# The last granule of the last MLP with tokens in rows, normed and stored block by block

## The chip, the cores and the metric

One core of one Trainium2 chip runs the whole program. The metric is the device time of one execution in microseconds. A difference is told here in microseconds and in per cent of the time before.

## What is computed

Two transformer-like stacks on 512 tokens of 1024 features, all in float32. The end of it, cut to what matters here, for the last layer:

```python
def rmsnorm(x, g):
    y = x * lax.rsqrt(jnp.mean(x * x, axis=-1, keepdims=True) + EPS)
    return y * g

def sq_relu_mlp(hn, w1, w2):          # w1: 1024 x 4096, w2: 4096 x 1024
    return jnp.square(jax.nn.relu(hn @ w1)) @ w2

h = h + sq_relu_mlp(rmsnorm(h, norm_mlp_g[l]), mlp_w1[l], mlp_w2[l])
return rmsnorm(h, final_norm_g)       # out: 512 tokens x 1024 features
```

## The kernel before

Every product is made three times: each operand is split in a high part (rounded to the fp32r type by ACT) and a low part (the rest, by DVE or POOL), and PE adds high x high, low x high, high x low in a PSUM bank (`split_sum`, L529 to L531).

**Layout.** The residual `x` (named `resid` in the trace) lies with features in rows: 8 tiles of 128 features x 512 tokens. The eight PSUM banks are four tile banks, used in turn, two `s_bank`, `pt_bank` (also `col_bank`) and `o_bank` (also `stat_bank`).

**The MLP.** The 4096 inner features are worked in 8 granules of 512. A granule is two up halves (`by_feature`, two tiles of 24 products each), whose result DVE scales (L1760) and ACT squares twice (L2270 into `t_buf`, L2271 as `g_hi`), and DVE subtracts (`g_lo`, L1175). Then `down` multiplies the granule back: first the quarter of the weights for output tiles 0 to 3, then the one for tiles 4 to 7, each tile 12 products. DVE adds each bank into `x` (L1223). All PE work for up half n+1 runs ahead of `down` for granule n.

**Weights.** SP loads them in chunks of 1 MB, in turn into the two slots of `raw`. ACT converts a chunk to `w_hi` in two pieces (`split_high`, L1921), DVE makes `w_lo` of the first piece (L1161) and, in this part of the program, POOL of the second (L499). `w_hi` and `w_lo` have two slots as well: chunk c may be converted only when PE is done with chunk c-2. For the last down quarter, that is the last up half.

**The end.** After each of the last `down`'s tiles, ACT squares the residual (L1933) and multiplies it by the final gain into `y_final` (L1946), and DVE adds up the squares (`add_squares`, L1792). Then `last_stat` sums them over the features on PE by a product with ones (L1107, L1112), ACT takes the root (L1954), DVE the reciprocal (L1886). `turned` transposes `y_final` on PE into eight banks of 128 tokens x 512 features (L1127), DVE and ACT scale four each into `out_stage` (L1892, L2348), and SP stores in four pieces of 512 KB (L416).

The order on each engine is the order of the code; engines meet by semaphores alone.

Of the kernel before, what the change touches and what calls it, by code (L numbers as in the profile page):

```python
# [14 lines left out]
P = 128  # L15
# [127 lines left out]
def build(nc, w, out):  # L143
# [5 lines left out]
    with ExitStack() as ctx:  # L149
# [3 lines left out]
        def sem(name):  # L153
            return ctx.enter_context(nc.semaphore(name))
# [56 lines left out]
        rope_a, rope_b = at(20480, S), at(20992, S)  # L211
        y_final, out_stage = at(4096, KT, S), at(8192, TT, D)
        OUT_PIECES = [(half, t) for half in range(2) for t in range(TT)]
        causal = biases.rearrange("p a b -> p (a b)")
# [71 lines left out]
        gm_ready = sem("gm_ready")  # L286
        y_ready = sem("y_ready")
        last_sq = sem("last_sq")
# [3 lines left out]
        out_scalar = sem("out_scalar")  # L292
        stored = sem("stored")
# [13 lines left out]

        def out_banks(tiles):

            four = [tile_bank[(tiles + q) % 4] for q in range(4)]  # L310
            return four + [s_bank[0], s_bank[1], o_bank, four[0]]

# [74 lines left out]
        def _(sp):  # L387
# [22 lines left out]

            for k in range(4):
                half, t = OUT_PIECES[2 * k]
                sp.wait_ge(out_vector, k + 1)
                sp.wait_ge(out_scalar, k + 1)
                cut = slice(512 * half, 512 * half + 512)
                sp.dma_start(out.rearrange("(t p) n -> p t n", p=P)[:, t:t + 2, cut], out_stage[:, t:t + 2, cut])\  # L416
                  .then_inc(stored, 16)
            sp.wait_ge(stored, 16 * 4)

# [83 lines left out]
        def _(pe):  # L503
# [40 lines left out]

            def by_feature(tiles=2, moving=None, arrive=None, first=0, pair=False, between=None):

                wait_chunk()
                for j in range(first, tiles):
                    dst = next_bank()[:]
                    parts = (range(0, 5), range(5, KT)) if j == 1 and between else (range(KT),)  # L550
# [475 lines left out]

            def mlp():
# [71 lines left out]
            back(3)  # L1099
            mlp()  # L1100

            def last_stat():

                pe.wait_ge(acc_ready, stats.n + 1)
                pe.wait_ge(std_done, stats.n)
                for t in range(TT):
                    nc.tensor.matmul(col_bank[:, t:t + 1], sq[:, 0, P * t:P * t + P], ones[:, 0:1], start=(t == 0), stop=False)  # L1107
                turned(0)
                for t in range(TT):
                    if t % 2 == 0:  # L1110
                        pe.wait_ge(last_sq, t // 2 + 1)
                    last = nc.tensor.matmul(col_bank[:, t:t + 1], sq[:, KT - 1, P * t:P * t + P], ones[:, 0:1],  # L1112
                                            start=False, stop=(t == TT - 1))
                last.then_inc(stat_full, 1)
                stats.n += 1

            def turned(q):

                half, t = OUT_PIECES[q]
                if t == 0:  # L1120
                    pe.wait_ge(y_ready, 4 * half + 4)
                if q < 4:
                    pe.wait_ge(tile_taken, tile.n - 3 + q + (q == 3))
                elif q == 7:
                    pe.wait_ge(out_vector, 1)
                for n in range(4):
                    last = nc.tensor.transpose(out_banks(tile.n)[q][:, P * n:P * n + P],  # L1127
                                               y_final[:, 4 * half + n, P * t:P * t + P], ident[:])
                last.then_inc(out_full, 1)

            last_stat()
            for q in range(1, len(OUT_PIECES)):
                turned(q)


        @block.vector
        def _(dve):
# [615 lines left out]
            def mlp(following):  # L1753
# [20 lines left out]
                if following:  # L1774
                    down(following)
                    return
                for n in range(KT - 1):
                    back_tile(n)
                    if n >= 2:
                        add_squares(n - 1)  # L1780
                add_squares(KT - 2)
                dve.wait_ge(tile_full, tile.n + 1)
                for cut in (slice(0, 256), slice(256, 512)):
                    ins = V.tensor_tensor(x[:, KT - 1, cut], tile_bank[tile.n % 4][:, cut], x[:, KT - 1, cut], ALU.add)
                    ins.then_inc(tile_taken, 1)
                tile.n += 1

            def add_squares(n):

                dve.wait_ge(sq_done, sq_n.n + n + 1)  # L1790
                settle()
                ins = V.tensor_tensor(sq[:, 0, :], sq[:, 0, :], sq[:, n, :], ALU.add)  # L1792
                if n < KT - 2:
                    keep_order(ins)
                else:
                    ins.then_inc(acc_ready, 1)

# [85 lines left out]

            stats.n += 1
            dve.wait_ge(std_done, stats.n)
            V.reciprocal(rstd_col[:, 0:4], rstd_col[:, 0:4]).then_inc(t_made, 1)  # L1886
            made.n += 1
            dve.wait_ge(t_made, made.n)
            for q in range(0, len(OUT_PIECES), 2):
                half, t = OUT_PIECES[q]  # L1890
                dve.wait_ge(out_full, q + 1)
                V.tensor_scalar(out_stage[:, t, 512 * half:512 * half + 512], out_banks(tile.n)[q][:],  # L1892
                                rstd_col[:, t:t + 1], None, ALU.mult).then_inc(out_vector, 1)


        @block.scalar
        def _(act):
# [41 lines left out]
            def prep(n, name, s=None):  # L1939
# [4 lines left out]
                squares(sq if s is None else s, n, x[:, n, :])  # L1944
                if not name:
                    A(y_final[:, n, :], x[:, n, :], ACT.Copy, scale=gain("final_norm_g_2", n)).then_inc(y_ready, 1)  # L1946

# [21 lines left out]
            def down(last=False, name=None, then=lambda: None):  # L1969

                for n in range(KT):
                    if last and not name and n == KT - 1:
                        for j in range(2):
                            cut = slice(256 * j, 256 * j + 256)
                            if j == 0:
                                taken()
                            else:
                                act.wait_ge(tile_taken, tile.n + 1)
                            A(sq[:, n, cut], x[:, n, cut], ACT.Square).then_inc(last_sq, 1)
                        A(y_final[:, n, :], x[:, n, :], ACT.Copy, scale=gain("final_norm_g_2", n)).then_inc(y_ready, 1)  # L1980
                    elif last:
# [282 lines left out]
            def mlp(following):  # L2264
                root(rstd[:, 0, :], None, stat_bank[:], None, D)

                def up(granule):
                    for j in range(2):
                        taken()
                        A(t_buf[:, j, :], r_buf[:, j, :], ACT.Square)  # L2270
# [6 lines left out]
                for n in range(7):  # L2277
                    down()
                    up(0)
                    up(1)  # L2280
                    if following and n == 5:
                        for j, table in enumerate((rope_cos, rope_sin)):
# [3 lines left out]
                            acts.n += 1  # L2286
                down(True, following)

# [49 lines left out]
            tile.n += 24  # L2338
            back(True, "mlp1")
            mlp(None)  # L2340

            root(None, rstd_col[:, 0:4], None, col_bank[:, 0:4], D)
            made.n += 1
            act.wait_ge(t_made, made.n)
            for q in range(1, len(OUT_PIECES), 2):
                half, t = OUT_PIECES[q]
                act.wait_ge(out_full, q + 1)
                A(out_stage[:, t, 512 * half:512 * half + 512], out_banks(tile.n)[q][:], ACT.Copy,  # L2348
                  scale=rstd_col[:, t:t + 1]).then_inc(out_scalar, 1)

# [40 lines left out]
```

## Time and profile before

| | us |
|---|---|
| median of 3 runs | 2001.6 |
| lowest, highest | 1999.96, 2001.6 |
| profiled execution | 1999.41 |
| its span | 1997.7 |
| PE busy | 1979.9 (99%) |
| DVE busy | 1162.7 (58%) |
| ACT busy | 756.3 (38%) |
| POOL busy | 247.9 (12%) |

A 128x512 matmul record is 0.39 us long, but the next one starts well before it ends, so records overlap and PE counts as busy throughout. Times in the timeline are microseconds from the start of the span, first the start, then the duration (of a merged group: from its first start to its last end). `PEclk` is the granted clock of TensorE, 1.00 being 2.4 GHz.

### The profile page before, as it was taken

The page shows a single profiled execution, that of the slowest core. Times are in us where ns is not written, and L with a number is a line of the kernel's source. Part 1 is how long each engine was busy: PE and PEld are TensorE (multiplying, and loading weights), DVE is VectorE, ACT ScalarE, POOL GpSimd, SP SyncE. Part 2 cuts the span into 40 slices and gives each one's busy share as a digit, 9 for nine tenths or more (in the row PEclk, how much of TensorE's full clock was granted, in tenths as well). Part 3 has the DMA queues.
Part 4 walks back from the last instruction along what each step waited for, and adds up shares of the span by engine and source line. Part 5 has one row for each costly group of instructions (what it writes and reads, how often), then busy time and mean ns, then how long its engine had stood idle before and what let it go on. Part 6 is the DMA issues. An engine that isn't in the chain of part 4 may idle for free.

```text
span 1997.7 us, 23016 instructions
## 1 busy us (share of the span) xinstructions
PE 1979.9 (99%) x9343; PEld 1623.4 (81%) x9343; DVE 1162.7 (58%) x1677; ACT 756.3 (38%) x1191; POOL 247.9 (12%) x189
## 2 busy tenths in 40 slices
PE   9999999999999999999999999999999999999998
PEld 7877777888888888888888888888877778888887
DVE  6665687577665656647577444443587674333334
ACT  5453554344333333533324323223443353232224
POOL 1001440000000000000001132222211012222221
PEclk9999999999999999999999999999999999999999
DMA  5322212113232322332222322323232013323321
GB/s 178 107 79 85 85 64 85 64 64 106 85 106 86 105 93 99 105 98 93 92 79 88 106 95 95 105 88 102 74 93 92 22 43 106 106 84 106 103 87 63
DMA packets 138713, 180.51 MB, mean 90 GB/s; under 512 B 9712, under 2 KB 97392, under 8 KB 138608
## 3 DMA queue, kind: packets, MB, share of 16 engines
q1 hardware_dynamic: 136720, 177.52, 27.3%
q8 instruction: 74, 1.21, 0.3%
q10 hardware_dynamic: 1632, 1.51, 0.2%
q14 instruction: 31, 0.25, 0.0%
q0 software_dynamic: 256, 0.02, 0.0%
HBM read 176.91 MB, written 2.10 MB: 90 GB/s over the span
## 4 chain that ended last, share of the span: by engine, by line
PE 94%; DVE 3%; issue 1%; ACT 1%; DMA 0%; POOL 0%; SPq 0%; ACTq 0%; POOLq 0%; DVEq 0%
PE bank L529 26%; PE bank L531 26%; PE bank L530 26%; PE bank L693 4%; PE bank L572 2%; PE bank L574 2%; PE bank L573 2%; PE bank L685 1%; PE bank L783 1%; PE bank L771 1%; PE bank L998 1%; DVE w_lo L1161 1%; DVE arena L1200 1%; PE bank L775 0%; DVE h_lo L1177 0%
## 5 line engine op out<-in xcount | busy, mean ns | idle before, releaser
L529 PE MATMUL bank<-h_hi,w_hi 128*128 128x512 f32 x1384 | 546.3, 395 | 0.0
L531 PE MATMUL bank<-h_hi,w_lo 128*128 128x512 f32 x1384 | 539.0, 389 | 0.0
L530 PE MATMUL bank<-h_lo,w_hi 128*128 128x512 f32 x1384 | 538.7, 389 | 0.0
L1921 ACT ACTIVATE w_hi<-raw 128x1024 fp32r<-128x1024 f32 (+2 forms) x335 | 331.2, 1031 | 507.6 <-PE bank L531 452.2
L529 PE MATMUL bank<-g_hi,w_hi 128*128 128x512 f32 (+1 forms) x972 | 377.1, 388 | 1.4 <-issue 0.7
L531 PE MATMUL bank<-g_hi,w_lo 128*128 128x512 f32 (+1 forms) x972 | 371.8, 383 | 0.0
L530 PE MATMUL bank<-g_lo,w_hi 128*128 128x512 f32 (+1 forms) x972 | 371.4, 382 | 0.0
L499 POOL TENSOR_TENSOR w_lo<-raw,w_hi 128x1024 fp32r<-128x1024 f32 (+1 forms) x75 | 181.9, 2426 | 1491.5 <-ACT w_hi L1921 1491.5
L1161 DVE TENSOR_TENSOR w_lo<-raw,w_hi 128x1024 fp32r<-128x1024 f32 (+2 forms) x258 | 308.9, 1221 | 60.2 <-ACT w_hi L1921 59.5
L1223 DVE TENSOR_TENSOR resid<-bank,resid 128x512 f32<-128x512 f32 x287 | 194.2, 688 | 224.9 <-PE bank L531 224.3
L529 PEld LDWEIGHTS bank<-h_hi,w_hi 128*128 128x128 f32 x1384 | 259.8, 188 | 56.3 <-issue 3.2
L530 PEld LDWEIGHTS bank<-h_lo,w_hi 128*128 128x128 f32 x1384 | 259.9, 188 | 55.8 <-issue 2.9
L531 PEld LDWEIGHTS bank<-h_hi,w_lo 128*128 128x128 f32 x1384 | 259.8, 188 | 54.4
L529 PEld LDWEIGHTS bank<-g_hi,w_hi 128*128 128x128 f32 x972 | 182.7, 188 | 39.3 <-issue 4.0
L531 PEld LDWEIGHTS bank<-g_hi,w_lo 128*128 128x128 f32 x972 | 182.6, 188 | 35.8
L530 PEld LDWEIGHTS bank<-g_lo,w_hi 128*128 128x128 f32 x972 | 182.8, 188 | 34.2 <-issue 0.2
L1760 DVE SCALAR_TENSOR_TENSOR arena<-bank,rstd 128x512 f32<-128x512 f32 x64 | 44.0, 691 | 179.0 <-PE bank L531 178.8
L2270 ACT ACTIVATE arena<-arena 128x512 f32<-128x512 f32 x64 | 40.5, 633 | 225.9 <-DVE arena L1760 225.9
L2012 ACT ACTIVATE arena<-bank 128x128 f32<-128x128 f32 (+3 forms) x104 | 44.7, 430 | 138.4 <-PE bank L685 137.8
L1175 DVE TENSOR_TENSOR g_lo<-arena,g_hi 128x512 fp32r<-128x512 f32 x112 | 74.9, 688 | 22.2 <-ACT g_hi L2271 20.6
L693 PE MATMUL bank<-arena 128*128 128x128 f32 (+2 forms) x448 | 84.0, 326 | 1.7 <-ACT arena L2029 0.9
L693 PEld LDWEIGHTS bank<-arena 128*128 128x128 f32 x448 | 66.6, 191 | 18.3 <-issue 5.6
(244 smaller groups left out, 1794.6 us busy)
## 6 DMA issues: line engine op xcount, KB each, us to landing
raw<-w SPq DMA_DIRECT2D x64, 1024.0 KB, 5.2
raw<-w_up SPq DMA_DIRECT2D x22, 1024.0 KB, 5.1
raw<-a_w_in SPq DMA_DIRECT2D x16, 1024.0 KB, 5.3
raw<-w_in SPq DMA_DIRECT2D x11, 1024.0 KB, 5.3
raw<-w_down SPq DMA_DIRECT2D x11, 1024.0 KB, 5.0
raw<-w_mkv SPq DMA_DIRECT2D x8, 1024.0 KB, 5.2
raw<-a_w_out SPq DMA_DIRECT2D x8, 1024.0 KB, 5.0
raw<-w_out SPq DMA_DIRECT2D x4, 1024.0 KB, 5.1
```

Source lines behind the costliest of these rows:

```text
L499: G.tensor_tensor(lo, src, hi.bitcast(F32), ALU.subtract).then_inc(w_split_pool, 1)
L529: nc.tensor.matmul(dst, a_hi, b_hi, start=(k == 0), stop=False)
L530: nc.tensor.matmul(dst, a_hi, b_lo, start=False, stop=False)
L531: last = nc.tensor.matmul(dst, a_lo, b_hi, start=False, stop=(k == n - 1))
L693: ins = nc.tensor.matmul(dst, a, b, start=first, stop=last)
L1161: V.tensor_tensor(lo, src, hi.bitcast(F32), ALU.subtract).then_inc(w_split, 1)
L1175: V.tensor_tensor(lo, src, hi.bitcast(F32), ALU.subtract).then_inc(ready, 1)
L1223: take(lambda b: V.tensor_tensor(x[:, n, :], b[:], x[:, n, :], ALU.add))
L1760: take(lambda b: V.scalar_tensor_tensor(r_buf[:, j, :], b[:], 0.0, rstd[:, 0, :], ALU.max, ALU.mult))
L1921: A(hi, src, ACT.Copy).then_inc(w_hi_done, 1)
L2012: A(prob_t_of(kind, u)[:, 0:nk], pt_bank[:, 0:nk], ACT.Copy).then_inc(pt_taken, 1)
L2270: A(t_buf[:, j, :], r_buf[:, j, :], ACT.Square)
```

## The change

1. The last granule's `down` is replaced by `last_granule`. The products have tokens in rows: `g` (128 tokens) is the stationary operand, 512 columns of the weights move. There are eight banks, block t of 128 tokens x half of the features, 12 products each; blocks 0 and 1 are made in two passes over the inner features, blocks 2 and 3 in one. Before its first product PE waits for both quarters' low parts.
2. The residual, which is complete up to the granule before, is turned on PE ahead of it (`residual`): 16 transposes between the two tiles of the last up half, 16 after them. ACT copies each bank into `x_rows`, four copies ahead of the second tile of the last up half and four after the last conversion of weights.
3. The end is done for each block of 128 tokens: DVE adds bank and `x_rows`, and multiplies by the gain; ACT squares the sum with `accum_out`, takes the root; DVE takes the reciprocal, scales and releases the store.
4. The gain comes in by its own DMA, spread over all partitions, on ACT's queue ahead of the last MLP. SP stores three blocks of 512 KB and the last in two of 256 KB.
5. The sums of squares on PE, `y_final`, the transposes at the end and ACT's scaling go.

```diff
+            def residual(first):
+                if first == 0:
+                    pe.wait_ge(std_done, stats.n)
+                    pe.wait_ge(tile_taken, tile.n - 3)
+                else:
+                    pe.wait_ge(x_rows_taken, 4)
+                for q in range(4):
+                    for n in range(4):
+                        last = nc.tensor.transpose(free_banks[q][:, P * n:P * n + P],
+                                                   x[:, 4 * (q % 2) + n, P * (first + q // 2):P * (first + q // 2) + P], ident[:])
+                    last.then_inc(x_turned, 1)
+            def last_granule():
+                def products(t, half, ks):
+                    dst, slot = out_bank(tile.n, t, half)[:], (chunk.n + half) % 2
+                    for k in ks:
...
+                        nc.tensor.matmul(dst, a_hi, b_hi, start=(k == 0), stop=False)
+                        nc.tensor.matmul(dst, a_hi, b_lo, start=False, stop=False)
+                        last = nc.tensor.matmul(dst, a_lo, b_hi, start=False, stop=(k == 3))
...
+                pe.wait_ge(w_split, by_vector(chunk.n + 2))
+                pe.wait_ge(w_split_pool, by_pool(chunk.n + 2))
+                for ks in ((0, 1), (2, 3)):
+                    for t in range(2):
+                        for half in range(2):
...
+                            products(t, half, ks)
+                for t in range(2, TT):
+                    for half in range(2):
+                        pe.wait_ge(x_rows_taken, 2 * t + half + 1)
+                        products(t, half, range(4))
...
-                    by_feature()
-                    down()
+                    by_feature(between=lambda: residual(0), first_part=KT) if last and n == 6 else by_feature()
+                    if last and n == 6:
+                        residual(2)
+                        last_granule()
+                    else:
+                        down()
...
# DVE, in place of add_squares, the reciprocal and four scalings
+            for t in range(TT):
+                for half in range(2):
+                    dve.wait_ge(out_full, 2 * t + half + 1)
...
+                    V.tensor_tensor(out_stage[:, t, cut], out_bank(tile.n, t, half)[:], x_rows[:, t, cut],
+                                    ALU.add).then_inc(last_added, 1)
...
+                    V.tensor_tensor(x_rows[:, t, cut], out_stage[:, t, cut],
+                                    last_gain[...], ALU.mult).then_inc(last_scaled, 1)
+                    if half == 0:
+                        dve.wait_ge(row_squared, 2 * t + 1)
+                        V.tensor_scalar(row_means[:, t:t + 1], row_sums[:, 2 * t:2 * t + 1], 1.0 / D, EPS, ...)
+                dve.wait_ge(row_std, t + 1)
+                keep_order(V.reciprocal(row_stds[:, t:t + 1], row_stds[:, t:t + 1]))
+                settle()
+                for half in range(2):
+                    V.tensor_scalar(out_stage[:, t, cut], x_rows[:, t, cut], row_stds[:, t:t + 1], None, ALU.mult)
...
# ACT
+                def rows_of_x(first):
+                    for q in range(4):
+                        act.wait_ge(x_turned, 2 * first + q + 1)
+                        A(x_rows[:, first + q // 2, cut], free_banks[q][:], ACT.Copy).then_inc(x_rows_taken, 1)
...
+                    A(last_squares[:, half, :], out_stage[...], ACT.Square, accum_out=row_sums[:, q:q + 1])
+                A(row_stds[:, t:t + 1], row_sums[:, 2 * t + 1:2 * t + 2], ACT.Sqrt, scale=1.0 / D,
+                  bias=row_means[:, t:t + 1]).then_inc(row_std, 1)
```

PE at the end of the last up half and the start of the last granule, before (L529 to L531 are the three products; `h` is the up half's operand, `g` the granule's):

```order
L529 MATMUL bank<-h_hi,w_hi 128x512
L530 MATMUL bank<-h_lo,w_hi 128x512
L531 MATMUL bank<-h_hi,w_lo 128x512
L529 MATMUL bank<-g_hi,w_hi 128x512
L530 MATMUL bank<-g_lo,w_hi 128x512
L531 MATMUL bank<-g_hi,w_lo 128x512
```

The same place now (L536 to L538 are the three products of the up half, L1045 the transposes, L1058 to L1060 the granule's products):

```order
L536 MATMUL bank<-h_hi,w_hi 128x512
L537 MATMUL bank<-h_lo,w_hi 128x512
L538 MATMUL bank<-h_hi,w_lo 128x512
L1045 MATMUL bank<-ident,resid 128x128 x16
L1058 MATMUL bank<-w_hi,g_hi 128x512
L1059 MATMUL bank<-w_lo,g_hi 128x512
L1060 MATMUL bank<-w_hi,g_lo 128x512
```

Sixteen transposes stand between the last up tile and the granule (the other sixteen one tile earlier), and the granule's first product has `g` stationary.

ACT from the last up half on, before (the waits are named in brackets; L1921 is the conversion of weights):

```order
L2270 ACTIVATE arena<-arena 128x512 [waits tile_taken]
L2271 ACTIVATE g_hi<-arena 128x512
L1921 ACTIVATE w_hi<-raw 128x1024 [waits tile_full,w_loaded1]
L1921 ACTIVATE w_hi<-raw 128x1024
L1933 ACTIVATE arena<-resid 128x512 [waits tile_taken]
L1946 ACTIVATE arena<-resid,vec 128x512
```

And now (L1934 is the conversion, L2273 the copies of turned residual, L2363 the squares, L2367 the root):

```order
L2273 ACTIVATE arena<-bank 128x512 [waits x_turned] x4
L2280 ACTIVATE arena<-arena 128x512 [waits tile_taken]
L2281 ACTIVATE g_hi<-arena 128x512
L1934 ACTIVATE w_hi<-raw 128x1024 [waits tile_full,w_loaded1]
L1934 ACTIVATE w_hi<-raw 128x1024
L2273 ACTIVATE arena<-bank 128x512 [waits x_turned] x4
L2363 ACTIVATE arena,rstd_col<-arena 128x512 [waits last_added] x2
L2367 ACTIVATE rstd_col<-rstd_col,small 128x1 [waits mean_ready,row_squared]
```

The conversion of the last chunk stands where it stood, with four copies ahead of the second tile's squares and four behind it.

DVE for one block of tokens, now (L1890 is the sum, L1893 the gain, L1898 the mean of the first half, L1906 the scalings):

```order
L1890 TENSOR_TENSOR arena<-bank,arena 128x512 [waits x_rows_taken,out_full]
L1893 TENSOR_TENSOR arena<-arena 128x512 [waits last_added]
L1898 TENSOR_SCALAR small<-rstd_col 128x1 [waits row_squared]
L1890 TENSOR_TENSOR arena<-bank,arena 128x512 [waits x_rows_taken,out_full]
L1893 TENSOR_TENSOR arena<-arena 128x512 [waits last_added]
L1901 RECIPROCAL rstd_col<-rstd_col 128x1 [waits row_std]
L1906 TENSOR_SCALAR arena<-arena,rstd_col 128x512 [waits last_scaled,own]
L1906 TENSOR_SCALAR arena<-arena,rstd_col 128x512 [waits last_scaled]
```

These eight stand four times, in place of the eight sums into `resid`, the sums of squares and four scalings from banks.

## Rows read from the trace of the kernel before

**Rows 1.** The page: span, and busy time of the engines.
```profile
span 1997.7 us, 23016 instructions
PE 1979.9 (99%) x9343; PEld 1623.4 (81%) x9343; DVE 1162.7 (58%) x1677; ACT 756.3 (38%) x1191; POOL 247.9 (12%) x189
```

**Rows 2.** Timeline of PE, first product of the last granule: start, us, what.
```profile
1964.93 0.39 PE L529 MATMUL bank<-g_hi,w_hi 128*128 128x512 f32 x1
```

**Rows 3.** Timeline of PE, last product, and the sums behind it.
```profile
1986.46 0.40 PE L531 MATMUL bank<-g_hi,w_lo 128*128 128x512 f32 x1
1986.69 0.95 PE L1107 MATMUL bank<-ones,arena 128*128 128x1 f32 x8
...
1987.97 0.95 PE L1112 MATMUL bank<-ones,arena 128*128 128x1 f32 x8
```

**Rows 4.** Chain of waits in order of time, its end: start, us, what.
```profile
1988.92 3.13 PE bank L1127 x28
...
1992.08 0.69 ACT arena L2348
```

**Rows 5.** Timeline of PE, transposes between products near the start.
```profile
14.40 0.39 PE L531 MATMUL bank<-h_hi,w_lo 128*128 128x512 f32 x1
14.63 0.60 PE L726 MATMUL bank<-ident,arena 128*128 128x128 f32 x4
...
15.30 0.39 PE L530 MATMUL bank<-h_lo,w_hi 128*128 128x512 f32 x1
```

**Rows 6.** Timelines of SP, ACT, DVE and POOL, the last chunk's load and split.
```profile
1948.10 0.37 SPq L409 DMA_DIRECT2D raw<-w  x1
...
1960.95 0.62 ACT L2271 ACTIVATE g_hi<-arena 128x512 fp32r<-128x512 f32 x1
...
1965.13 0.69 DVE L1760 SCALAR_TENSOR_TENSOR arena<-bank,rstd 128x512 f32<-128x512 f32 x1 [4.75 <-PE bank L531]
...
1966.91 1.99 ACT L1921 ACTIVATE w_hi<-raw 128x1024 fp32r<-128x1024 f32 x2
...
1968.98 2.48 POOL L499 TENSOR_TENSOR w_lo<-raw,w_hi 128x1024 fp32r<-128x1024 f32 x1 [8.39 <-ACT w_hi L1921]
```

**Rows 7.** Groups by line and shape, PE: weights moving: count, busy us, mean ns.
```profile
L572 PE MATMUL bank<-w_hi,h_hi 128*128 128x512 f32 x192 | 77.1, 401 | 0.0
```

**Rows 8.** Timeline of DVE: independent operations, then two that depend on each other.
```profile
1977.10 0.68 DVE L1223 TENSOR_TENSOR resid<-bank,resid 128x512 f32<-128x512 f32 x1
1977.70 0.68 DVE L1792 TENSOR_TENSOR arena<-arena 128x512 f32<-128x512 f32 x1
...
1544.62 0.15 DVE L1276 RECIPROCAL small<-small 128x1 f32<-128x1 f32 x1
1544.81 0.49 DVE L1278 TENSOR_SCALAR arena<-arena,small 128x512 f32<-128x512 f32 x1
```

**Rows 9.** ACT: timeline of a square with its sum; groups: root on one column.
```profile
27.30 1.04 ACT L2044 ACTIVATE arena<-arena 128x1024 f32<-128x1024 f32 x1
28.25 0.18 ACT L2044 ACTIVATION_READ_ACCUMULATOR arena<-arena 128x1 f32 x1
...
L2050 ACT ACTIVATE rstd_col<-small 128x1 f32<-128x1 f32 x1 | 0.2, 202 | 0.0
```

**Rows 10.** Line L416, the stores: issue to landing of the first, of the last.
```profile
DMA to landing us min/median/max: 2.8/2.8/2.8
DMA to landing us min/median/max: 4.4/4.4/4.4
```

**Rows 11.** Windows at the end: length, busy of each engine, clock, DMA share, GB/s.
```profile
1994.50:1995.40 0.90, 0.00 (x0) 0.00 (x0) 0.00 (x0) 0.00 (x0) 0.00 (x0) 1.00 1.01 373
...
1995.80:1997.70 1.90, 0.00 (x0) 0.00 (x0) 0.00 (x0) 0.00 (x0) 0.00 (x0) 0.50 0.50 190
```

**Rows 12.** Timeline of PE, the program's first records, and the same ones later.
```profile
1.34 3.78 PE L699 MATMUL bank<-ones 128*128 128x128 f32 x16 [1.34 <-POOL ones L430]
...
7.34 1.06 PE L699 MATMUL bank<-ones 128*128 128x128 f32 x8
```

More of the change, by code:

```diff
@@ L211, in build @@
         rope_a, rope_b = at(20480, S), at(20992, S)
-        y_final, out_stage = at(4096, KT, S), at(8192, TT, D)
-        OUT_PIECES = [(half, t) for half in range(2) for t in range(TT)]
+        last_gain, last_squares, out_stage, x_rows = at(4096, KT, P), at(5120, 2, S), at(8192, TT, D), at(12288, TT, D)
+        row_sums, row_means, row_stds = rstd_col[:, 4:12], small[:, 32:36], rstd_col[:, 0:4]
         causal = biases.rearrange("p a b -> p (a b)")
@@ L306, in gain, with out_bank @@
             return vec[:, c:c + 1]
-        def out_banks(tiles):
-            four = [tile_bank[(tiles + q) % 4] for q in range(4)]
-            return four + [s_bank[0], s_bank[1], o_bank, four[0]]
+        free_banks = [s_bank[0], s_bank[1], pt_bank, o_bank]
+        def out_bank(tiles, t, half):
+            last_four = [tile_bank[(tiles + q) % 4] for q in range(4)]
+            return (last_four + free_banks)[2 * t + half]
         UNITS = [(h, i) for h in range(8) for i in range(TT)]
@@ L543, in w_tiles, with by_feature @@
                 return [(view(w_hi, slot)[:, k, cut], view(w_lo, slot)[:, k, cut]) for k in range(n)]
-            def by_feature(tiles=2, moving=None, arrive=None, first=0, pair=False, between=None):
+            def by_feature(tiles=2, moving=None, arrive=None, first=0, pair=False, between=None, first_part=5):
                 wait_chunk()
@@ L549, in by_feature @@
                     dst = next_bank()[:]
-                    parts = (range(0, 5), range(5, KT)) if j == 1 and between else (range(KT),)
+                    parts = (range(0, 5), range(5, KT)) if j == 1 and between and first_part < KT else (range(KT),)
+                    if j == 1 and first_part == KT:
+                        between()
                     for part in parts:
@@ L1099, in _ @@
             back(3)
[L1100 to L1133, printed above, removed]
+            mlp(last=True)
         @block.vector
@@ L1775, in mlp @@
                     down(following)
[L1776 to L1796, printed above, removed]
             mlp("mix1")
@@ L1971, in down @@
                 for n in range(KT):
[L1972 to L1981, printed above, removed]
+                    if last:
                         taken()
@@ L2279, in mlp @@
                     up(0)
-                    up(1)
+                    up(1, last=not following and n == 6)
                     if following and n == 5:
@@ L2286, in mlp @@
                             acts.n += 1
[L2287 removed]
+                if following:
+                    down(True, following)
+                else:
+                    rows_of_x(2)
             act.dma_start(pos_i.bitcast(I32), w["positions_2"].partition_broadcast(P)).then_inc(pos_loaded, 16)
@@ L2339, in _ @@
             back(True, "mlp1")
+            first = sum(n for _, n in VECTORS[2][:-1])
+            act.dma_start(last_gain, w["vectors"][first:first + KT, 2, :].partition_broadcast(P)).then_inc(gain_loaded, 16)
             mlp(None)
[L2342 to L2349, printed above, removed]
+            for t in range(TT):
+                for half in range(2):
+                    q = 2 * t + half
+                    act.wait_ge(last_added, q + 1)
+                    if q >= 2:
+                        act.wait_ge(row_squared, q - 1)
+                    A(last_squares[:, half, :], out_stage[:, t, 512 * half:512 * half + 512], ACT.Square,
+                      accum_out=row_sums[:, q:q + 1]).then_inc(row_squared, 1)
+                act.wait_ge(row_squared, 2 * t + 2)
+                act.wait_ge(mean_ready, t + 1)
+                A(row_stds[:, t:t + 1], row_sums[:, 2 * t + 1:2 * t + 2], ACT.Sqrt, scale=1.0 / D,
+                  bias=row_means[:, t:t + 1]).then_inc(row_std, 1)
 def kernel(**inputs):
```

64 lines of the change are left out of this document (40 added, 24 removed).

## The prediction

> **What bounds the kernel now.** I read the page first: the span is 1997.7 us and PE is busy for 99% of it [rows 1], so a matmul added or a stall of PE costs its whole length, unless it falls after the last product. The change touches only the last granule and what follows, so the next view was the timeline of the end. There PE starts the last granule's products at 1964.93, in the slot right behind the last product of the second up half [rows 2], and its last product ends at 1986.46 + 0.40 = 1986.86 [rows 3]. What follows is a tail: squares, 32 transposes, root, reciprocal, scaling, four stores, until 1997.7. Tail: 10.84 us. The chain of waits gives the tail's first part to PE's own short matmuls (3.13 us for 28 transposes) and leaves ACT last, at 1992.77 [rows 4]. The rest is the store.
>
> The profiled execution took 1999.41 us, 1.71 more than its span; the median shown is 2001.6. I work out the difference on the span and add it to 2001.6.
>
> **Term 1, the transposes ahead of the granule.** 32 transposes of the residual now stand in the stream: 16 between the two tiles of the last up half, 16 behind them. Before, 32 stood in the tail, so their count is the same, only their place is new. The price between products is read at the start of the trace: from product 14.40 to product 15.30 there are 0.90 us for one product slot, four transposes and another slot [rows 5]; a slot is 0.2265 us (21.76 us from the first product at 1964.93 [rows 2] to what follows the last at 1986.69 [rows 3], over 96), so four transposes cost 0.447 us, 0.112 each. The last 28 in the tail say the same, 3.13 / 28 = 0.112 [rows 4]. Each 16 cost 1.78 us. The first 16 stand squarely on the path. Of the second 16 see term 2.
>
> **Term 2, a new wait for the second weight quarter.** Before, PE starts on the first quarter (512 of the 1024 output features) and needs the second only 48 products later, at 1964.93 + 48 x 0.2265 = 1975.8. In the new order the second quarter comes with the seventh product, and both waits stand ahead of the first, so PE waits for both to be split before it begins. The second quarter's weights have been loaded long since (issued 1948.10 [rows 6]), but its high part is written over the slot of the last up chunk, so ACT may not begin before the last up tile is done. [Rows 6] are that chain: tile taken by DVE at 1965.13, two squares on ACT, two conversions from 1966.91 to 1968.90, and POOL's low piece from 1968.98 to 1971.46. Before, this ended 4.3 us ahead of its use; now it is the last thing PE waits for. Everything in the chain hangs on the last up tile, which comes 1.78 later, so PE's first product starts at 1971.46 + 1.78 + 0.03 = 1973.27. That is 8.34 after 1964.93: 3.56 are the 32 transposes and 4.78 are idle slots. The second 16 transposes are therefore free, as they lie inside this wait; if the wait went, they would cost 1.78.
>
> ACT has four copies (bank to SBUF) ahead of the last up tile. It has time: the first tile's squares end at 1960.95 + 0.62 = 1961.6 [rows 6], four copies of at most 0.7 us (ACT's last operation, bank to SBUF too, took 0.69 [rows 4]) end by 1964.4, and the next tile comes at 1966.9. The other four stand behind the two conversions, off POOL's chain; they end by 1973.5, before their first use 10.9 us into the products.
>
> **Term 3, the products.** 96 products before, 96 after. The tokens are now the stationary operand, the weights move. The same form ran in the earlier projections, at a mean of 401 ns a record with the stage's own starts in it [rows 7], against 0.39 us a record here [rows 2]. I price it at the same 0.2265 a slot. The last product's record ends at 1973.27 + 95 x 0.2265 + 0.39 = 1995.18, which is 8.32 later than before.
>
> **Term 4, DVE beside the products.** For each token block DVE now adds twice, multiplies by the gain twice, makes one small sum, one reciprocal and two scalings; ACT squares twice with a row sum and takes one root. From rows: add or multiply 0.69 (0.61 from start to start where nothing is waited for), reciprocal 0.15, scaling from SBUF 0.49, and 0.04 between dependent instructions [rows 8]; a square of 512 columns 0.62 [rows 6], the read of a square's sum 0.18, overlapping it by 0.09, and a root on one column 0.20 [rows 9]. A block's first half takes 0.73 + 0.77 until the sum is there + 0.07 = 1.57 on DVE; its second half takes 0.73 + 0.77, root 0.22, reciprocal 0.20, scalings 0.85: 2.77. Together 4.34. The first four banks fill at 7.0, 8.35, 9.7 and 11.05 us after the first product, the others at 13.8, 16.5, 19.2 and 21.95. DVE starts at 7.0 and is free for the last bank at 7.0 + 3 x 4.34 + 1.57 = 21.6. It is ready 0.35 ahead of PE, no more. So three blocks hide beside the products and only the last half's chain is left, but every 0.1 us more per block uses that up.
>
> **Term 5, the new tail.** From the last product's end: 0.03, add 0.69, 0.03, square and its sum 0.71, 0.04, root 0.20, 0.04, reciprocal 0.15, 0.04, scalings 0.49 + 0.41 = 2.83. Then the store. Before, the first store of 512 KB, with nothing ahead of it, landed 2.8 after issue; the last, behind three others, 4.4, and the span ended 0.5 after it [rows 10]. The queues moved about 380 GB/s [rows 11], so 512 KB take 1.37 and the fixed part is 1.43. The new last store has 256 KB (0.68) behind another 256 KB issued 0.41 ahead of it: 1.43 + 0.68 + 0.27 = 2.4. Bounds: 2.1 with nothing ahead, 4.4 as the last store of before took, which had 1.5 MB ahead of it; I stay near the first. New tail: 2.83 + 0.05 + 2.4 + 0.5 = 5.8, against 10.84: 5.06 less.
>
> **Sum.** +8.32 - 5.06 = +3.26: the span comes to about 2001.0 and the median to 2004.8. The saved tail is real, but the wait for the split costs more.
>
> **The gain's load** (512 KB, on ACT's queue ahead of the last MLP) costs nothing: it is issued where ACT next waits for PE's sum of squares, and ACT is busy for 38% of the span [rows 1]. Without that cover it would be one issue, 0.37 us on SP [rows 6].
>
> **The clock.** PE's new gap is 4.6 us between records. The one fall of the granted clock in the trace stands at the end: PE's last work ends at 1992.05 [rows 4], the clock is 1.00 until 1995.4 and 0.50 from 1995.8 on [rows 11], so it fell 3.4 to 3.7 us after. The gap is longer than that.
> The Trainium skill (TensorE: Matmul & The Clock Gate, Part 4: PE-mode transpose) says that transposes do not count as PE-busy for the clock gate. By that rule the second 16 transposes would lengthen the quiet stretch to 6.4 us and the fall would be near certain. The trace speaks against it: nothing but transposes ran after 1988.92 [rows 3, 4], and the clock was full for another 6.5 us. So I leave the rule out of the sum; by it the time would be that of the first rival.
>
> **The rivals.**
> - *The clock falls in the new gap.* PE restarts at 1.2 GHz instead of 2.4. What a slow stretch looks like is seen at the start: 16 records from 1.34 take 3.78 us, 8 of the same from 7.34 take 1.06 [rows 12], so it is half rate, for some 4.4 us of work until about 5.7. Half of 4.4 is lost: 2.2, bounds 1 and 3.5. For it: the gap exceeds the 3.7 us within which it fell. Against: that is one observation, and the margin is 0.9 us. +5.5 in all: 2007.0, slower by more than 0.2%. This is the case on the other side of the bound, and it decides once the fall comes before 1973.3.
> - *DVE is late for the last bank.* If dependent steps take 0.1 to 0.15 longer than my rows (the row sum on a square, the waits on an instruction of the same engine), a block takes some 4.8, the last add begins 1.1 late and the last chain is 0.3 longer: +1.4, 2006.2.
> - *The wait does not come*, because the second quarter is split sooner or taken later than I read. Then the idle slots go and the 32 transposes alone delay the products: 3.26 - 4.78 = -1.5, 2000.1. Against it: both waits stand ahead of the first product, and the slot is the last up chunk's.
>
> **How the numbers follow.** Less than 0.2%, 4 us here, can't be told from no change. Forecast 0.50, clock 0.33, DVE late 0.10, no wait 0.07. The forecast lies only 0.8 below the bound of 4; a fifth of its chance is beyond it (0.10), of the clock's five sixths (0.28), of DVE's six tenths (0.06): slower 0.44. Faster by over 0.2% would need 7 us less than the forecast, more than the wait and the doubt of the store together: 0.02. Same: 0.54. The likeliest case alone spans 2003.4 to 2006.0; the range, 2002.2 to 2008.4, takes in the clock's case up to 3.5 lost.
>
> **What would show it.** PE idle for 4.5 to 4.8 us behind the second 16 transposes, with POOL's low piece named as what ended it; 96 products in 21.75 us behind it; granted clock 1.00 through (or 0.50 for some us: the first rival); the last product to the end of the span in 5.8 us; DVE idle for some tenths before its last add. Wrong would be: a wait under 3 us, a slot over 0.2265 in the new form at full clock, a last store over 3 us to land.

## The result, and the profile after

| | before | after |
|---|---|---|
| median, us | 2001.6 (14 runs) | 2006.74 (14 runs) |
| lowest, highest | 1999.56, 2001.9 | 2005.13, 2007.38 |
| profiled execution, its span | 1999.41, 1997.7 | 2007.1, 2005.3 |

The ratio is 1.0027, 95% interval 1.0021 to 1.0034: slower by 0.27%, or 5.1 us between medians. That is more than the 3.2 of the forecast and nearly the 5.5 of the first rival; 2006.74 lies in the range.

The timeline of the changed kernel, PE and the engines it waits for, from the last up tile on (start, duration, what, and in brackets the idle time before it and what ended it):

```profile
1969.00 1.91 PE L1045 MATMUL bank<-ident,resid 128*128 128x128 f32 x16
...
1969.20 0.69 DVE L1781 SCALAR_TENSOR_TENSOR arena<-bank,rstd 128x512 f32<-128x512 f32 x1 [6.52 <-PE bank L538]
...
1970.98 1.99 ACT L1934 ACTIVATE w_hi<-raw 128x1024 fp32r<-128x1024 f32 x2
...
1973.04 2.43 POOL L506 TENSOR_TENSOR w_lo<-raw,w_hi 128x1024 fp32r<-128x1024 f32 x1 [10.18 <-ACT w_hi L1934]
...
1975.58 0.77 PE L1058 MATMUL bank<-w_hi,g_hi 128*128 128x512 f32 x1 [4.67 <-issue]
1976.14 0.63 PE L1059 MATMUL bank<-w_lo,g_hi 128*128 128x512 f32 x1
...
1979.56 0.60 PE L1058 MATMUL bank<-w_hi,g_hi 128*128 128x512 f32 x1
1979.98 0.41 PE L1059 MATMUL bank<-w_lo,g_hi 128*128 128x512 f32 x1
...
1999.29 0.39 PE L1060 MATMUL bank<-w_hi,g_lo 128*128 128x512 f32 x1
```

They answer to [rows 6] and [rows 2, 3]. Behind the second 16 transposes PE is idle for 4.67 us. The page puts this down to "issue", that is, to nothing it can show, but POOL's low piece ends at 1973.04 + 2.43 = 1975.47, 0.11 before PE starts. Then the records are 0.63 long and 0.43 apart, until 1980.0, where they fall back to 0.39 and 0.23. The windows name the cause (the column before the last two is the granted clock):

```profile
1966.00:1969.00 3.00, 3.00 (x15) 2.40 (x15) 0.00 (x0) 0.00 (x0) 0.00 (x0) 1.00 0.00 0
1969.00:1973.10 4.10, 1.91 (x17) 1.67 (x15) 3.03 (x4) 3.18 (x5) 0.06 (x1) 1.00 0.00 0
1973.20:1979.90 6.70, 4.32 (x10) 3.47 (x11) 0.08 (x1) 1.71 (x4) 2.28 (x1) 0.50 0.01 2
1980.00:1999.00 19.00, 19.00 (x85) 15.73 (x84) 12.47 (x26) 5.61 (x16) 0.00 (x0) 1.00 0.14 59
```

The clock fell in the gap, and the first ten products ran at 1.2 GHz. From the start of the first product to that of the last are 23.71 us; 95 slots of 0.2265 are 21.52. The clock cost 2.19. How much of a low clock is paid depends on how much of it lies beside work: it was low for 6.8 us here, 2.4 of them still in the gap.

The end of the changed kernel, timeline of ACT, DVE and SP for the last half of the last block:

```profile
1999.72 0.69 DVE L1890 TENSOR_TENSOR arena<-bank,arena 128x512 f32<-128x512 f32 x1 [0.18 <-PE bank L1060]
...
2000.44 0.63 ACT L2363 ACTIVATE arena<-arena 128x512 f32<-128x512 f32 x1 [1.10 <-DVE arena L1890]
...
2000.98 0.19 ACT L2363 ACTIVATION_READ_ACCUMULATOR arena<-arena 128x1 f32 x1
2001.20 0.29 ACT L2367 ACTIVATE rstd_col<-rstd_col,small 128x1 f32<-128x1 f32 x1
2001.52 0.17 DVE L1901 RECIPROCAL rstd_col<-rstd_col 128x1 f32<-128x1 f32 x1 [0.39 <-ACT rstd_col L2367]
2001.72 0.88 DVE L1906 TENSOR_SCALAR arena<-arena,rstd_col 128x512 f32<-128x512 f32 x2
2002.24 0.81 SPq L424 DMA_DIRECT2D out<-arena  x2
```

The line of the last stores gives `2.0/2.2/2.3` us from issue to landing for 256 KB each, against 2.8 to 4.4 for 512 KB each in [rows 10]. From the end of PE's last record (1999.68) to the end of the span are 5.6 us, 10.84 before.

The profiled execution carries one thing more that is not the change's. PE reaches the last up tile 2.3 us later than in the profile of before, with 1.78 of transposes taken off: the clock fell once more, near 232 us, in a stretch that both kernels share. Windows there, the kernel before and the changed one:

```profile
232.00:240.00 8.00, 6.76 (x38) 5.07 (x39) 7.66 (x12) 4.70 (x14) 4.32 (x8) 1.00 0.40 132
...
232.40:239.20 6.80, 6.04 (x20) 4.27 (x21) 5.36 (x8) 2.25 (x6) 2.42 (x5) 0.50 0.46 154
```

Up to 231 us the changed kernel's DVE is 0.4 us behind that of before, from 245 us on it is 2.3 behind: 0.4 was there already and 1.9 came with the fall. So traces are compared from a point behind it: from DVE's taking of the last up tile to the end of the span, before 1997.7 - 1965.13 = 32.57, after 2005.3 - 1969.20 = 36.10, and 1.78 for the transposes ahead of it. **The change costs 5.31 us**: 8.36 for the later start of the products (predicted 8.34), 2.19 for the clock, and 5.24 won in the tail (predicted 5.06).

### The profile page after: what moved, and what is told of

Its sections match the earlier page's. It is cut to its first block, busy times and chain, and to the rows that moved or that the text cites. A ratio compares the mean times of both kernels' runs of the same rounds, so it can differ in the third digit from the quotient of the medians.

```text
span 2005.3 us, 23011 instructions
## 1 busy us (share of the span) xinstructions
PE 1983.8 (99%) x9327; PEld 1625.7 (81%) x9327; DVE 1166.2 (58%) x1689; ACT 754.4 (38%) x1197; POOL 244.9 (12%) x189
## 4 chain that ended last, share of the span: by engine, by line
PE 94%; DVE 3%; issue 1%; ACT 1%; POOL 0%; ACTq 0%; DVEq 0%; POOLq 0%
PE bank L536 25%; PE bank L538 25%; PE bank L537 25%; PE bank L702 4%; PE bank L581 2%; PE bank L583 2%; PE bank L582 2%; PE bank L694 1%; PE bank L792 1%; PE bank L780 1%; PE bank L1007 1%; DVE w_lo L1182 1%; DVE arena L1221 1%; PE bank L784 1%; PE bank L1058 0%
## 5 line engine op out<-in xcount | busy, mean ns | idle before, releaser
L536 PE MATMUL bank<-h_hi,w_hi 128*128 128x512 f32 x1384 | 546.3, 395 | 0.2 <-DVE h_lo L1198 0.2
L538 PE MATMUL bank<-h_hi,w_lo 128*128 128x512 f32 x1384 | 539.1, 390 | 0.0
L1934 ACT ACTIVATE w_hi<-raw 128x1024 fp32r<-128x1024 f32 (+2 forms) x335 | 331.2, 1031 | 507.2 <-PE bank L538 452.1
L536 PE MATMUL bank<-g_hi,w_hi 128*128 128x512 f32 (+1 forms) x940 | 364.6, 388 | 1.4 <-issue 0.7
L538 PE MATMUL bank<-g_hi,w_lo 128*128 128x512 f32 (+1 forms) x940 | 359.3, 382 | 0.0
L537 PE MATMUL bank<-g_lo,w_hi 128*128 128x512 f32 (+1 forms) x940 | 359.0, 382 | 0.0
L1244 DVE TENSOR_TENSOR resid<-bank,resid 128x512 f32<-128x512 f32 x280 | 189.5, 688 | 217.0 <-PE bank L538 216.2
L536 PEld LDWEIGHTS bank<-h_hi,w_hi 128*128 128x128 f32 x1384 | 259.9, 188 | 56.6 <-issue 3.6
L538 PEld LDWEIGHTS bank<-h_hi,w_lo 128*128 128x128 f32 x1384 | 259.7, 188 | 54.5
L536 PEld LDWEIGHTS bank<-g_hi,w_hi 128*128 128x128 f32 x940 | 176.7, 188 | 38.0 <-issue 4.0
L538 PEld LDWEIGHTS bank<-g_hi,w_lo 128*128 128x128 f32 x940 | 176.6, 188 | 34.6
L537 PEld LDWEIGHTS bank<-g_lo,w_hi 128*128 128x128 f32 x940 | 176.8, 188 | 33.0 <-issue 0.2
```

Source lines behind the costliest of these rows:

```text
L536: nc.tensor.matmul(dst, a_hi, b_hi, start=(k == 0), stop=False)
L537: nc.tensor.matmul(dst, a_hi, b_lo, start=False, stop=False)
L538: last = nc.tensor.matmul(dst, a_lo, b_hi, start=False, stop=(k == n - 1))
L1244: take(lambda b: V.tensor_tensor(x[:, n, :], b[:], x[:, n, :], ALU.add))
L1934: A(hi, src, ACT.Copy).then_inc(w_hi_done, 1)
```

## The experiments

In the table, "distance" is that from DVE's taking of the last up tile to the end of the span, and "net" is distance + 1.78 - 32.57, the part of the change and its variant in that one trace. Each value of distance and net is from one trace. Ratios are against runs of the kernel before on the same chip: the first four variants against 33 runs with a median of 2001.16, the last three against 27 with 2001.01.

| kernel | distance | net | median, ratio and interval |
|---|---|---|---|
| the change | 36.10 | +5.3 | 2006.74, 1.0027 (1.0021 to 1.0034) |
| first quarter first | 29.13 | -1.7 | 1998.60, 0.9988 (0.9980 to 0.9997) |
| gap filled, products | 34.13 | +3.3 | 2004.37, 1.0015 (1.0006 to 1.0024) |
| gap filled, transposes | 34.03 | +3.2 | 2004.11, 1.0015 (1.0006 to 1.0024) |
| low piece by DVE | 34.34 | +3.6 | 2004.04, 1.0018 (1.0009 to 1.0027) |
| wait at the seventh | 34.30 | +3.5 | 2004.71, 1.0018 (1.0009 to 1.0027) |
| first quarter first, no transposes | 28.66 | -3.9 (without 1.78) | 1997.38, 0.9983 (0.9974 to 0.9992) |
| first quarter first, early fill | 29.13 | -1.7 | 1997.79, 0.9986 (0.9977 to 0.9994) |

### The first quarter first

```diff
-                pe.wait_ge(w_split, by_vector(chunk.n + 2))
-                pe.wait_ge(w_split_pool, by_pool(chunk.n + 2))
-                for ks in ((0, 1), (2, 3)):
+                pe.wait_ge(w_split, by_vector(chunk.n + 1))
+                pe.wait_ge(w_split_pool, by_pool(chunk.n + 1))
+                for half in range(2):
+                    if half == 1:
+                        pe.wait_ge(w_split, by_vector(chunk.n + 2))
+                        pe.wait_ge(w_split_pool, by_pool(chunk.n + 2))
                     for t in range(2):
-                        for half in range(2):
...
-                            products(t, half, ks)
+                        pe.wait_ge(tile_taken, tile.n - 3 + 2 * t + half)
+                        products(t, half, range(4))
```

DVE waits for the banks in their new order.

> The changed kernel, with the granule's products in another order: the first quarter's columns of blocks 0 and 1 first (24 products, 5.4 us), waiting for the first quarter alone, then a wait for the second quarter and their other columns; blocks 2 and 3 as before. Theory A (the wait for POOL's low piece and the clock that falls in it are the loss): PE's gap behind the second 16 transposes goes, the second quarter is ready before its product, the clock is 1.00 there; 4.8 + 2.2 us less than the changed kernel, so about 1.5 us under the kernel before. Theory B (the loss lies in the products with weights moving, or in DVE's chain beside them): within 1 us of the changed kernel.

Its timeline of PE and POOL:

```profile
1968.27 1.91 PE L1045 MATMUL bank<-ident,resid 128*128 128x128 f32 x16
...
1969.93 0.47 PE L1058 MATMUL bank<-w_hi,g_hi 128*128 128x512 f32 x1
...
1972.33 2.50 POOL L506 TENSOR_TENSOR w_lo<-raw,w_hi 128x1024 fp32r<-128x1024 f32 x1 [10.19 <-ACT w_hi L1935]
...
1991.58 0.39 PE L1060 MATMUL bank<-w_hi,g_lo 128*128 128x512 f32 x1
```

The products start in the transposes' next slot and run through in 21.65 us; POOL ends at 1974.83, 0.6 ahead of the 25th product. Net -1.7 where -1.5 was expected. The changed kernel's whole loss, and a little more, lay in the wait and in what the clock did in it. Theory B is out: the new form of the products and the new end are the same here. Against the kernel before, the median is 0.12% less and the ratio's interval ends at 0.9997, just under 1: faster, at the edge of what the runs can tell.

### The gap filled with products, and with transposes

```diff
+                pe.wait_ge(tile_taken, tile.n - 3)
+                for _ in range(19):
+                    nc.tensor.matmul(out_bank(tile.n, 0, 0)[:, 0:P], ones[:], ones[:], start=True, stop=True)
                 pe.wait_ge(w_split, by_vector(chunk.n + 2))
```

(in the other run `for _ in range(38): nc.tensor.transpose(out_bank(tile.n, 0, 0)[:, 0:P], x[:, 0, 0:P], ident[:])`)

> The changed kernel, with 19 products of ones (128 columns, two records each, 4.2 us) put on PE between the second 16 transposes and the wait for the split, into a bank that the granule overwrites. Theory A: the wait ends when it did, the clock stays at 2.4 GHz, the products take 21.75 us from first to last slot and the time falls by the clock's 2.2 us. Theory B (the slow start of the products has another cause, such as new weights or the stage's start): no change from the changed kernel, or 0 to 0.3 us more.

> As the run with 19 products of ones, with 38 transposes of 128 columns (4.3 us) in their place. Theory A (PE's work of any kind holds the clock, as the 28 transposes at the end of the kernel before seemed to): clock 1.00, 2.2 us less than the changed kernel. Theory C (transposes do not count for the clock, as the page on TensorE says, and the clock fell since the last product had ended 4 us before): the clock falls as in the changed kernel, no gain.

Timeline of PE with products as filler:

```profile
1969.02 4.41 PE L1066 MATMUL bank<-ones 128*128 128x128 f32 x38
1973.87 0.47 PE L1058 MATMUL bank<-w_hi,g_hi 128*128 128x512 f32 x1 [0.44 <-issue]
...
1995.53 0.39 PE L1060 MATMUL bank<-w_hi,g_lo 128*128 128x512 f32 x1
```

and with transposes, with the clock of the products' start:

```profile
1969.12 4.31 PE L1066 MATMUL bank<-ident,resid 128*128 128x128 f32 x38
1973.98 0.47 PE L1058 MATMUL bank<-w_hi,g_hi 128*128 128x512 f32 x1 [0.56 <-issue]
```

```profile
1969.00:1973.80 4.80, 4.43 (x41) 4.19 (x39) 1.92 (x2) 4.28 (x7) 2.37 (x1) 1.00 0.01 3
1973.90:1980.00 6.10, 6.02 (x27) 5.02 (x28) 0.00 (x0) 0.00 (x0) 0.00 (x0) 1.00 0.00 0
```

Both hold the clock; the products run in 21.66 us, and the net is +3.3 and +3.2. That is the forecast's own case, +3.26, with the clock taken out of it: the wait alone costs what I had worked out, and the clock 2.0 to 2.1 on top. Theory B and theory C are both out. The rule of the Trainium skill (TensorE: Matmul & The Clock Gate, Part 4: PE-mode transpose), that transposes do not count as busy, does not hold for these: from the last product of the up half to the first of the granule are 6.4 us with transposes alone in them, and the clock stayed at 2.4 GHz. A second sign is in the times: the changed kernel's fourteen runs lie between 2005.13 and 2007.38, the 22 filled ones, in another series, between 2003.31 and 2005.17.

### The last low piece by DVE

```diff
-        SHARED = [c >= NOT_SHARED and c not in MLA_OUT for c in range(len(CHUNKS))]
+        SHARED = [c >= NOT_SHARED and c not in MLA_OUT and c < len(CHUNKS) - 1 for c in range(len(CHUNKS))]
```

> The changed kernel, with the second low piece of the last chunk on DVE and not on POOL. Theory A: DVE makes it from 0.08 before its first piece ends, in 1.23 us, 1.1 us ahead of POOL; PE's gap shrinks from 4.7 to 3.6 us and the time by 1.1 if the clock still falls, by 3.3 if it no longer does. Theory B (something else ends the wait): no change.

Timelines of DVE and PE, and the window of low clock:

```profile
1969.72 2.36 DVE L1182 TENSOR_TENSOR w_lo<-raw,w_hi 128x1024 fp32r<-128x1024 f32 x2 [0.25 <-ACT w_hi L1934]
...
1972.13 0.80 PE L1058 MATMUL bank<-w_hi,g_hi 128*128 128x512 f32 x1 [3.56 <-DVE w_lo L1182]
```

```profile
1971.80:1975.10 3.30, 2.97 (x7) 2.41 (x8) 0.28 (x1) 0.78 (x2) 0.00 (x0) 0.50 0.00 0
```

The gap is 3.56 and now the page names its releaser, the low piece. The clock fell here as well, 3.2 us after the last transpose ended (1968.57), for a shorter time: 23.07 us from the first to the last product, so 1.55 lost. Net that is 1.7 less than the changed kernel, where 1.1 was expected with a fall, since the fall cost 0.6 less. Its eleven runs lie between 2002.11 and 2006.6, wider than any other kernel's: it may be that with a shorter gap the clock falls in some executions and not in others (full clock would give +2.2 net, about 2001.7). That isn't shown: only one execution was traced, and none of the eleven has a mean clock above 0.999.

### The wait moved to the seventh product

```diff
-                pe.wait_ge(w_split, by_vector(chunk.n + 2))
-                pe.wait_ge(w_split_pool, by_pool(chunk.n + 2))
+                pe.wait_ge(w_split, by_vector(chunk.n + 1))
+                pe.wait_ge(w_split_pool, by_pool(chunk.n + 1))
...
+                            if ks[0] == 0 and t == 0 and half == 1:
+                                pe.wait_ge(w_split, by_vector(chunk.n + 2))
+                                pe.wait_ge(w_split_pool, by_pool(chunk.n + 2))
```

> The changed kernel in its own order, with the wait for the second quarter moved from ahead of the first product to ahead of the seventh, the first that uses it. Theory A: six products (1.36 us) run in front of POOL's piece and nothing else moves, so the gap stands behind them, 3.2 us long; 1.4 us less than the changed kernel where the clock falls in it, 3.6 less where it does not. Rival D (placing the wait ahead of its need was the mistake): the whole 4.7 + 2.2 us come back, as in the run with the first quarter first.

Timeline of PE, then two windows:

```profile
1971.29 0.40 PE L1060 MATMUL bank<-w_hi,g_lo 128*128 128x512 f32 x1
...
1974.98 0.47 PE L1058 MATMUL bank<-w_hi,g_hi 128*128 128x512 f32 x1 [3.29 <-issue]
```

```profile
1975.00:1975.60 0.60, 0.60 (x3) 0.52 (x4) 0.00 (x0) 0.00 (x0) 0.00 (x0) 1.00 0.00 0
1975.70:1979.00 3.30, 3.30 (x9) 2.52 (x9) 0.00 (x0) 0.00 (x0) 0.00 (x0) 0.50 0.03 5
```

Six products went ahead of the piece and 3.29 us of gap remained. Here the clock fell 0.7 us after PE had restarted, and cost 1.75, so that 1.8 came back where 1.4 was expected with a fall. Nine runs lie between 2003.69 and 2005.66; two, at 2001.29 and 2001.31, had a clock of 1.00 throughout. Against the lowest run of before in the same series (1999.4, clock 1.00 too) these two are 1.9 us up, which is 3.26 less the 1.36 of six products. That the clock fell in this gap in each of the other nine is worked out from their times and mean clocks; one was traced. Rival D is out: it is the order of the products, not the place of the wait, that covers POOL's piece.

### Without the transposes

```diff
-                for q in range(4):
-                    for n in range(4):
-                        last = nc.tensor.transpose(free_banks[q][:, P * n:P * n + P], ...)
-                    last.then_inc(x_turned, 1)
...
-                        act.wait_ge(x_turned, 2 * first + q + 1)
...
-                        A(x_rows[:, first + q // 2, cut], free_banks[q][:], ACT.Copy)...
+                        A(x_rows[:, first + q // 2, cut], x[:, q, :], ACT.Copy)...
```

> The run with the first quarter first, without the 32 transposes of the residual (ACT copies tiles of the residual as they lie, so the output is not the reference's). Term 1 of the prediction: 3.6 us less than with them, 0.11 us each, since no wait hides any of them there. Rival: PE's transposes are partly hidden behind POOL's split of the second quarter, and less than 2 us come back.

Timelines of PE and DVE, with the first, the tenth and the last of the granule's products:

```profile
1966.64 0.39 PE L1053 MATMUL bank<-w_hi,g_hi 128*128 128x512 f32 x1
...
1966.84 0.69 DVE L1777 SCALAR_TENSOR_TENSOR arena<-bank,rstd 128x512 f32<-128x512 f32 x1 [4.75 <-PE bank L538]
...
1969.50 0.50 PE L1053 MATMUL bank<-w_hi,g_hi 128*128 128x512 f32 x1 [0.35 <-DVE g_lo L1192]
...
1989.48 0.39 PE L1055 MATMUL bank<-w_hi,g_lo 128*128 128x512 f32 x1
```

DVE's idle time before the last up tile is 4.75 again, not 6.51 to 6.52 with transposes: 1.77 for the first 16. But net it is -3.9, only 2.25 less than with the transposes and not 3.56. The products take 22.84 us here, 1.3 more than their slots: without the second 16 transposes PE catches up with DVE's low half of `g` (0.35 and a smaller gap) and, at the 25th product, with POOL's piece (it starts at 1973.31, POOL ends at 1973.21). So with this order of the products the first 16 transposes cost their 1.77 and the second 16 only some 0.5, as other waits take their place. My expectation was 1.3 too high; the rival was nearer, though the 2.25 are above its 2, and more of the 1.3 stands at DVE's part than at POOL's. The medians are no help: they lie 1.2 us apart, in two series of runs.

### The early fall of the clock

```diff
+                if piece == 16:
+                    pe.wait_ge(tile_taken, mem_values_first + 2 * half + tok - 3)
+                    keep_busy(9, tile_bank[(mem_values_first + 2) % 4])
```

`keep_busy(n, bank)` makes n products of ones into a bank; the change that lets it take the bank is not shown, nor is the order of the products, which is that of the run with the first quarter first.

> The run with the first quarter first, and nine products of ones in a gap of 2.1 us far ahead of the change, near 231 us, where the clock fell in the traces of the changed kernel and of three of its variants, and not in that of the kernel before. If that fall is what sets executions of one kernel 1 to 2.5 us apart, the clock stays full there and the executions lie together near the lowest of that run, 1998.1 to 1998.4; the median falls by 0.3 to 1 us. If not, median and spread stay.

Before the fill PE waited 2.10 us at this place; the timeline has now, in the same place:

```profile
229.87 0.31 PE L694 MATMUL bank<-ident,arena 128*128 128x128 f32 x1 [0.59 <-DVE arena L1297]
230.02 2.17 PE L708 MATMUL bank<-ones 128*128 128x128 f32 x18
```

The clock is 1.00 up to the end of the last product. Ten of eleven runs lie between 1997.2 and 1998.31 (one at 2001.71), with clocks of 0.999 and 1.00, where the run without the fill had 1998.12 to 2000.23, four of the eleven with 0.998. The median is 0.8 us lower, in another series of runs, and the ratio to before 0.9986 against 0.9988, whose intervals overlap. That the fill keeps the clock full at this place is shown for the traced execution; that it takes most of the spread away is likely from the clocks, not shown, and its gain in the median is not clear of noise. It has the lowest median of the kernels that do the whole computation.

## Why the prediction was right and wrong

- **Term 1, transposes at 0.112 each: right.** DVE's idle time before the last up tile grew from 4.75 to 6.52, by 1.77. That the second 16 lie inside the wait held too.
- **Term 2, the wait for the second quarter: right**, 4.67 us of gap, a start 8.36 later. The run with the first quarter first shows that the wait was the cause, and the one with DVE's low piece that POOL's length sets it. The prediction expected the page to name POOL's low piece as what ended the wait; it did not, and the 0.11 us between the two and that run speak for it instead.
- **Term 3, 0.2265 a slot with weights moving: right**, where the clock is full: 21.65 us from first to last start against 21.52.
- **Term 4, DVE ready just in time: right**, though by 0.18 where 0.35 was forecast. With its small sum done at 1999.5 and the last bank full at 1999.7, DVE waited 0.18. From the second block's first add (1989.18) to its second (1990.73) are 1.55 us, and to the next block's (1993.54) 2.81, against 1.57 and 2.77. That rival did not happen.
- **Term 5, the new tail: right**, 5.6 against 5.8; the root took 0.29 and not 0.20, the last store landed in 2.3 and not 2.4.
- **The clock: wrong.** "Forecast 0.50, clock 0.33" had the two the wrong way round. The mechanism and its price were in the rival (2.2 forecast, 2.19 measured), the sum of the rival was 5.5 and the trace gives 5.31. That the price came out to a hundredth is luck in part. It was taken from the length of work at a low rate at the start, 4.4 us; the window of that stretch gives a granted clock of 1.00, so the low clock there was read from the spacing of the records alone:

```profile
1.30:5.10 3.80, 3.76 (x17) 3.77 (x18) 0.00 (x0) 1.49 (x2) 1.68 (x9) 1.00 0.75 233
```

  The falls at the shorter gaps of two variants cost 1.55 and 1.75. What failed is the step that turned the one fall in the trace of before into a margin: "the gap exceeds the 3.7 us within which it fell", with a margin of 0.9. The delay after PE's last work is no fixed figure. It was 2.3 us in the changed kernel (transposes end at 1970.91, 0.50 from 1973.2), 3.2 with DVE's low piece, up to 3.7 before, and in the run with the wait at the seventh product the fall came after the restart, 4.0 us after the product ahead of the gap. The ends of the nine traces settle it. PE rests there after its last product, and the clock fell 2.2, 2.3, 2.4, 2.9, 3.5, 3.7, 4.0, 4.2 and 4.4 us after it. The longest is that of the run with the early fill (last product's end 1989.97), the shortest that of the gap filled with products (1995.92):

```profile
1990.00:1994.30 4.30, 0.00 (x0) 0.00 (x0) 2.43 (x5) 1.02 (x3) 0.00 (x0) 1.00 0.26 97
...
1998.10:2001.60 3.50, 0.00 (x0) 0.00 (x0) 0.74 (x2) 0.00 (x0) 0.00 (x0) 0.50 0.40 150
```

  So the 3.7 was one draw out of a scatter of more than 2 us, and a margin over a single draw says little about the chance. The gap of 4.67 is longer than all nine. All 14 runs of the changed kernel lie over 2005.1, 2.3 and more above 1999.56 + 3.26, so by the times the fall came in every one. In hindsight a gap of 4.7 us counts as a fall, not as a chance of one in three; the one trace at hand couldn't say so.
- **The order of chances.** The time forecast, 2004.8, is that of the two filled runs (2004.11, 2004.37); the 2006.74 measured is that of the rival (2007.0). The measured time lies in the range because the range took in the rival, not because the forecast's own case held.

What gives the change its worth came out as worked out too: the end for each block saves 5.2 us, the transposes cost 3.6, and the difference of 1.7 is what the run with the first quarter first shows. The 3.6 is the time of the transposes; without them only 2.25 came back.

## What to carry to other kernels

When products are put in another order, list for each operand the time it becomes ready and the first product that now needs it; an operand that was made 4.3 us early may have become the last. PE's gaps of 3.3 us and more cost more than their length in every trace here, though not in every execution: price such a gap with the slow clock behind it, and fill it if it can't be closed. Put first the products whose operands are ready, here one half of the columns, and the same work is 7 us faster.

## What the runs showed of the hardware

- After PE's last work the clock fell at no fixed time: 2.3 to 4.0 us after it in the gaps before the granule, 2.2 to 4.4 at the ends of the nine traces, at times after work had begun again, and it stayed low for 3.3 to 6.8 us. In the traces it fell in every gap of 3.3, 3.6 and 4.7 us. By clocks and times, which is an inference, it fell in nine of eleven executions with the 3.3 us gap and in all fourteen with 4.7; for 3.6 the times don't decide.
- In a gap of 2.1 us with light work on both sides, near 231 us, it fell in six of eight traces, in four of them 0.6 to 1.3 us after PE's last record and in two after the restart. PE then came to the last up tile some 0.6 to 2.3 us later than in the trace of before, transposes taken off.
- Transposes and short float32 products hold the clock alike: 4.3 and 4.4 us of them, clock 1.00.
- Beside POOL's low piece, DVE's multiply of two SBUF operands took far longer, while the sum right ahead of it, of a PSUM bank and an SBUF operand, did not. In the run with the first quarter first:

```profile
1973.02 0.69 DVE L1891 TENSOR_TENSOR arena<-bank,arena 128x512 f32<-128x512 f32 x1 [0.47 <-PE bank L1060]
1973.75 1.63 DVE L1894 TENSOR_TENSOR arena<-arena 128x512 f32<-128x512 f32 x1
```

  The multiply takes 0.69 elsewhere. POOL ran from 1972.33 to 1974.83, and the multiply ended 0.55 us after it. It did the same in the run without transposes (2.19 long) and in the one with the early fill (1.62). It looks as if it had waited for POOL to be done; no run isolates this. It lies off the path there, but it would not in a tighter order.
